# Opening of a hybrid mixer layer on one core: own slots for the rows of x, split loads, and one conditioning chunk multiplied on TensorE

## The reference

```
mod = c @ w_ada + b_ada                       # 6 x 1024: sh1, sc1, gt1, sh2, sc2, gt2
h   = rms_norm(x, g_mix) * (1 + sc1) + sh1
a, conv, linear, stick, gate_logits = split(h @ w_in)
merged = sum of sigmoid(gate_i) * branch_i     # window attention, convolution, GLA, stick-breaking
x = x + gt1 * (merged @ w_out)
h = rms_norm(x, g_mlp) * (1 + sc2) + sh2
x = x + gt2 * (relu(h @ w_up)**2 @ w_down)
```

## Time and profile before

| | |
|---|---|
| median of three runs | 1986.41 us (1985.16 to 1990.21) |
| the profiled execution | 1990.35 us, its span 1988.6 us |
| TensorE busy | 1927.7 us, 97% of the span |
| VectorE, ScalarE, GpSimd busy | 1191.7, 831.3, 227.2 us |
| bytes moved by DMA | 266.24 MB, mean 134 GB/s |
| mean granted TensorE clock | 0.992 |

### The profile page before, as it was taken

The page is one execution under the profiler, slowest core; times in us unless marked ns, Lnnn a source line. Parts: engine busy times, 40 slices in busy tenths (PEclk is TensorE's granted clock), DMA queues, the critical chain, the costliest instruction groups (busy, mean ns, idle before and its releaser), DMA issues. The chain is left out here.

```text
span 1988.6 us, 24178 instructions
## 1 busy us (share of the span) xinstructions
PE 1927.7 (97%) x9224; PEld 1551.3 (78%) x9224; DVE 1191.7 (60%) x1555; ACT 831.3 (42%) x1314; POOL 227.2 (11%) x136
## 2 busy tenths in 40 slices
PE   5999999999999999998999999999999999999999
PEld 4787888878766667876788788788788887888887
DVE  6545757101256666727657478667766765678855
ACT  5411111223466633164656255333455445444443
POOL 0121121211121225212101000000000000000000
PEclk9999999999999999999999999999999999999999
DMA  8345554323311242244122576501353546963343
GB/s 268 109 142 152 154 164 133 100 86 111 129 56 48 64 166 67 94 175 161 51 87 71 167 259 221 190 11 39 110 164 128 170 149 217 318 201 108 98 118 101
DMA packets 229004, 266.24 MB, mean 134 GB/s; under 512 B 12010, under 2 KB 157546, under 8 KB 228890
## 3 DMA queue, kind: packets, MB, share of 16 engines
q1 hardware_dynamic: 228720, 264.63, 42.0%
q10 hardware_dynamic: 170, 0.07, 0.0%
HBM read 187.46 MB, written 77.20 MB: 133 GB/s over the span
## 5 line engine op out<-in xcount | busy, mean ns | idle before, releaser
L663 PE MATMUL dn_ps<-h_hi,dn_hi 128*128 128x512 f32 (+1 forms) x1120 | 453.5, 405 | 16.0 <-ACT dn_out L156 5.1
L665 PE MATMUL dn_ps<-h_hi,dn_lo 128*128 128x512 f32 (+1 forms) x1120 | 440.2, 393 | 0.0
L664 PE MATMUL dn_ps<-h_lo,dn_hi 128*128 128x512 f32 (+1 forms) x1120 | 439.9, 393 | 0.0
L663 PEld LDWEIGHTS dn_ps<-h_hi,dn_hi 128*128 128x128 f32 (+1 forms) x1120 | 210.9, 188 | 84.2 <-issue 33.7
L156 ACT ACTIVATE dn_out<-dn_ps 128x512 f32<-128x512 f32 (+1 forms) x138 | 81.7, 592 | 424.1 <-PE dn_ps L665 402.8
L139 POOL TENSOR_TENSOR dn_lo<-dn_raw,dn_hi 128x1024 fp32r<-128x1024 f32 (+1 forms) x69 | 172.3, 2498 | 663.8 <-ACT dn_hi L135 663.8
L665 PEld LDWEIGHTS dn_ps<-h_hi,dn_lo 128*128 128x128 f32 (+1 forms) x1120 | 210.5, 188 | 47.9
L664 PEld LDWEIGHTS dn_ps<-h_lo,dn_hi 128*128 128x128 f32 (+1 forms) x1120 | 210.9, 188 | 43.1 <-issue 1.2
L1227 ACT ACTIVATE tl_ring_hi<-tl_cell 128x512 fp32r<-128x512 f32 x112 | 70.6, 630 | 140.7 <-PE mg_ps_y L665 126.5
L664 PE MATMUL mg_ps_y<-tl_ring_lo,tl_ring_hi 128*128 128x512 f32 x320 | 124.6, 389 | 0.0
L663 PE MATMUL mg_ps_y<-tl_ring_hi,tl_ring_hi 128*128 128x512 f32 x320 | 124.6, 389 | 0.0
(11 more groups left out here) (420 smaller groups left out, 3719.1 us busy)
## 6 DMA issues: line engine op xcount, KB each, us to landing
dn_raw<-w_in_dram SPq DMA_DIRECT2D x70, 512.0 KB, 4.3
tl_raw_hidden<-hidden SPq DMA_DIRECT2D x112, 256.0 KB, 2.7
ada<-w_ada_dram SPq DMA_DIRECT2D x24, 1024.0 KB, 8.0
proj<-dn_out SPq DMA_DIRECT2D x72, 256.0 KB, 2.3
logits<-dn_out SPq DMA_DIRECT2D x64, 256.0 KB, 2.3
tl_unit<-w_up_dram SPq DMA_DIRECT2D x64, 256.0 KB, 3.2
hidden<-tl_hidden_sum SPq DMA_DIRECT2D x16, 1024.0 KB, 4.9
tl_cell<-w_down_dram SPq DMA_DIRECT2D x64, 256.0 KB, 5.1
```

The costliest lines, as they stand in the source:

```text
L663: nc.tensor.matmul(out, w_hi[:, t, :], x_hi[:, t, :], start=begin, stop=False, skip_group_check=reopened)
L664: nc.tensor.matmul(out, w_hi[:, t, :], x_lo[:, t, :], start=False, stop=False, skip_group_check=reopened)
L665: mm = nc.tensor.matmul(out, w_lo[:, t, :], x_hi[:, t, :], start=False, stop=end, skip_group_check=reopened)
```

## The change

- Each row tile of x has a slot of its own: four in the old place, four in the space that the low part of h takes later (`x_lent`). No load of x waits.
- ScalarE's queue issues c and six of the vectors before `root(0)`; the other seven loads are issued by SP between x's fifth tile and the first chunk.
- A chunk is loaded in two halves of four pieces each, with a semaphore each.
- GpSimd scales rows 1 to 5 (`x_pooled`), VectorE rows 0, 6 and 7.
- Chunk 1 is not chained on VectorE: TensorE multiplies its 32 blocks of 128x128 by the columns of c and accumulates them in PSUM (`direct`), 16 blocks ahead of `opening(0)` and 16 behind it, where `sum_chunk(1)` stood. Chunks 0, 2 and 3 are chained as before.
- On ScalarE the splits of the first weight tiles move behind the roots, the third into the loop over f. On VectorE chunk 0's chain, the vectors' copies, `modulation(0)` and `scale_columns(0)` move ahead of the last takes, and the low parts of the first weight tiles behind them.

```
-X_RING = 4
+X_OWN = 4
+X_ON_POOL = 5
...
+    PART = KT // 2
+    DIRECT = ((1, 0), (1, 1))
...
+        x_lent = nc.alloc_sbuf_tensor_at("x_lent", [P, S // P - X_OWN, D], F32, offset=k.h_base + 3 * KT * S * 2)
...
+            def load_chunk(n, part):
+                slot, rows = n % ADA_RING, slice(part * PART, (part + 1) * PART)
+                if n >= ADA_RING and part == 0:
+                    sp.wait_ge(ada_direct, direct_until(n - ADA_RING))
+                    if chained(n - ADA_RING):
+                        sp.wait_ge(ada_step, steps_until(n - ADA_RING))
...
+            for tt in range(1, X_ON_POOL + 1):
+                pool.wait_ge(x_rooted, tt + 1)
+                nc.gpsimd.tensor_scalar(x_rows(tt), x_rows(tt), rinv_x[:, tt:tt + 1], None, ALU.mult).then_inc(x_pooled, 1)
...
+            root(0)
+            root(1)
+            root(2)
+            take(0)
+            root(3)
+            take(1)
...
+            root(7)
+            take(5)
+            dense.split(act, 0)
+            take(6)
+            dense.split(act, 1)
+            take(7)
             for f in range(KT):
...
+                if f == 0:
+                    act.wait_ge(turned, 2 * TT)
                 nc.scalar.activation(k.h_hi[:, f, :], xn[:, f, :], ACT.Identity, **affine).then_inc(h_hi_ready, 1)
...
+                if f == 0:
+                    dense.split(act, 2)
...
+            def direct(n, part):
+
+                pe.wait_ge(ada_in[2 * (n % ADA_RING) + part], 32 * (n // ADA_RING + 1))
+                if n >= 1:
+                    pe.wait_ge(mod_ready, n)
+                closes = not chained(n)
+                for i, first in enumerate(CHUNKS[n]):
+                    for m in range(ADA_COLS):
+                        for kt in range(part * PART, (part + 1) * PART):
+                            opens = part == 0 and i == 0 and m == 0 and kt == 0
+                            last = nc.tensor.matmul(ps_m[:, first + m:first + m + 1], ada[:, n % ADA_RING, kt, i, m * P:(m + 1) * P],
+                                                    k.cols[:, V_C + kt:V_C + kt + 1], start=opens, stop=(closes and kt == KT - 1 and m == ADA_COLS - 1 and i == len(CHUNKS[n]) - 1))
+                last.then_inc(ada_direct, 1)
...
+            turn(5)
+            if chained(0):
+                sum_chunk(0)
+            turn(6)
+            turn(7)
+            if (1, 0) in DIRECT:
+                direct(1, 0)
             for f in range(KT):
                 opening(f)
-                if f % 2 == 0 and f // 2 + 1 < OPEN_CHUNKS:
+                if f == 0 and (1, 1) in DIRECT:
+                    direct(1, 1)
+                elif f % 2 == 0 and f // 2 + 1 < OPEN_CHUNKS:
                     sum_chunk(f // 2 + 1)
```

More of the change, by code:

```diff
@@ L235, in sum_after, with direct_until, chained, steps_until @@
         return load_step(i) + 2
+    def direct_until(n):
+        return sum(1 for chunk, part in DIRECT if chunk <= n)
+    def chained(n):
+        return [kt for kt in range(KT) if (n, kt // PART) not in DIRECT]
+    def steps_until(n):
+        return sum(len(chained(i)) for i in range(n + 1))
+    def sums_until(n):
+        return sum(1 for i in range(n + 1) if chained(i))
     with ExitStack() as ctx:
@@ L473, in sum_chunk @@
                         at = (i * ADA_COLS + m) * P
-                        last = nc.tensor.matmul(ps_m[:, first + m:first + m + 1], ada_sum[:, at:at + P], k.ones[:, 0:1], start=True, stop=True)
+                        last = nc.tensor.matmul(ps_m[:, first + m:first + m + 1], ada_sum[:, at:at + P], k.ones[:, 0:1], start=alone, stop=(alone or at == (len(CHUNKS[n]) * ADA_COLS - 1) * P))
                 last.then_inc(ada_done, 1)
+            def direct(n, part):
[10 more added lines that the diff above has]
+                last.then_inc(ada_direct, 1)
             def opening(f):
@@ L495, in _ @@
             pe.wait_ge(const_ready, 2)
-            for tt in range(TT):
-                turn(tt)
-                if tt == 1:
-                    pe.wait_ge(c_in, 16)
-                    nc.tensor.transpose(ps_v[:, 0:KT], c_rows[:, :], k.ident[0:KT, 0:KT]).then_inc(c_turned, 1)
+            turn(0)
+            pe.wait_ge(c_in, 16)
+            nc.tensor.transpose(ps_v[:, 0:KT], c_rows[:, :], k.ident[0:KT, 0:KT]).then_inc(c_turned, 1)
+            turn(1)
+            turn(2)
+            turn(3)
+            pe.wait_ge(c_taken, 1)
+            if (0, 0) in DIRECT:
+                direct(0, 0)
+            turn(4)
             pe.wait_ge(vec_in, 16 * n_vec)
-            pe.wait_ge(vec_taken, 1)
             nc.tensor.transpose(ps_v[:, 0:P], vec_rows[:, :], k.ident[:, :])
@@ L529, in scale_rows @@
                 dve.wait_ge(x_rooted, tt + 1)
-                nc.vector.tensor_scalar(x_rows[:, tt % X_RING], x_rows[:, tt % X_RING], rinv_x[:, tt:tt + 1], None, ALU.mult).then_inc(x_scaled, 1)
+                nc.vector.tensor_scalar(x_rows(tt), x_rows(tt), rinv_x[:, tt:tt + 1], None, ALU.mult).then_inc(x_scaled, 1)
             def take(tt):
@@ L539, in chain @@
                 late = n - OPEN_CHUNKS
-                if first == 0:
-                    if late >= 0:
-                        dve.wait_ge(late_in[late % LATE_RING], 16 * (late // LATE_RING + 1))
-                    else:
-                        dve.wait_ge(ada_in[n % ADA_RING], 32 * (n // ADA_RING + 1))
-                    if n >= 1:
-                        dve.wait_ge(ada_done, n)
-                for kt in range(first, last):
+                own = chained(n)
+                for at, kt in enumerate(own):
+                    if not first <= kt < last:
+                        continue
+                    if kt == own[0] and late >= 0:
+                        dve.wait_ge(late_in[late % LATE_RING], 16 * (late // LATE_RING + 1))
+                    if late < 0 and (kt == own[0] or kt == PART):
+                        dve.wait_ge(ada_in[2 * (n % ADA_RING) + kt // PART], 32 * (n // ADA_RING + 1))
+                    if kt == own[0] and sums_until(n) > 1:
+                        dve.wait_ge(ada_done, sums_until(n) - 1)
                     ck = k.cols[:, V_C + kt:V_C + kt + 1]
@@ L594, in _ @@
                     nc.vector.memset(k.headsum[64 * a:64 * a + 64, 64 * b:64 * b + 64], 1.0 if a == b else 0.0)
[L595 to L611 removed]
+            scale_rows(0)
+            dve.wait_ge(c_turned, 1)
+            nc.vector.tensor_copy(k.cols[:, V_C:V_C + KT], ps_v[:, 0:KT]).then_inc(c_taken, 1)
+            dve.wait_ge(c_taken, 1)
+            take(0)
+            take(1)
+            chain(0, 0, 1)
+            take(2)
+            chain(0, 1, 3)
+            take(3)
+            chain(0, 3, KT)
+            take(4)
+            scale_rows(6)
             dve.wait_ge(vec_turned, 1)
```

147 lines of the change are left out of this document (76 added, 71 removed).

## The result

Over 22 runs of each, the kernel after took 1991.21 us in the median (1986.05 to 1994.5) and the one before 1987.23 (1981.73 to 1991.66). The ratio is 1.0017, with a 95% interval of 1.0009 to 1.0025: the change makes this kernel slower by 0.17%, some 3.4 us (the medians lie 4.0 apart). Forecast were 1984.7 us, 1.7 less than before, in a range of 1980.3 to 1989.5. The profiled execution took 1994.22 us, its span 1992.4.

The account below looks back on a forecast made before the run. It took the opening's end to set the total: blocks from 27.9, plus 7.1, 6.4 and 4.4 us, put chunk 1's modulation at 45.8, a gain of 1.7. From the median 1986.41 that gave 1984.7 us, range 1980.3 to 1989.5.

Parts of the forecast that it names:

- What bounds the kernel: Whole kernel: TensorE is busy 494.75 of 500 us behind the opening, so only when the opening ends counts.
- A microsecond out of the opening is one out of the total: Behind the opening: the rest runs as long as before, so time saved in the opening shortens the total equally.
- h nine microseconds earlier: Ahead of the first product: h_hi at about 27.5 instead of 36.51, its low part at 31.2 instead of 40.20.
- Where the blocks start: TensorE's first blocks of chunk 1: start at 27.9 us, when the first half of chunk 1 has landed.
- the term of GpSimd's rows: Five row scalings in the opening: taken as 1.3 us each, hidden up to about 2.1, so zero in the sum.
- The rival with the other sign: GpSimd's five rows slow: blocks start at 15.9 + 5p, late from p = 2.4; at most 10.3 us slower; chance 0.06.
- Hidden, as forecast: VectorE in the opening: GpSimd's scalings may hold it 1.3 us each, covered by chunk 0's wait for its load.
- The level of the first sixteen blocks: Blocks ahead of opening(0): run at the low clock, 7.1 us, ending at 35.0.
- The second sixteen blocks: Blocks behind opening(0): run at the high clock, 4.4 us, ending at 45.8.
- its first rival: The clock falls in the second sixteen blocks: gain 1.7 becomes 0.4 or a loss up to 1.7; chance 0.32.
- the forecast's opening: Opening as a whole: chunk 1's modulation at 45.8 instead of 47.58, later periods unchanged, a gain of 1.7 us.

Follow-up runs that it names:

- rows_on_vector: Kernel after, with VectorE scaling all eight rows of x and GpSimd none; ratio to the kernel before 0.9998.
- second_chained: Kernel after, with the second half of chunk 1 chained on VectorE again instead of the second sixteen blocks; ratio to the kernel before 0.9987.
- fillers: Kernel after, with an unused product of 512 columns behind each of the second sixteen blocks; ratio to the kernel before 1.0026.
- eight_blocks: Kernel after, with VectorE scaling all rows, eight blocks of chunk 1 on TensorE and its other six pieces chained; ratio to the kernel before 0.9964.
- own_slots: Kernel before, with only eight own slots for the rows of x; ratio to the kernel before 1.0001.
- before_again: Kernel before, unchanged, timed and profiled once more; ratio to the kernel before 0.9994.
- all_chained: Kernel after, with chunk 1 chained entirely on VectorE and no blocks; ratio to the kernel before 0.9989.
- rows_vector_second_chained: Kernel after, with VectorE scaling all rows and chaining chunk 1's second half, first sixteen blocks kept; ratio to the kernel before 0.9985.

## Why the prediction was wrong

**What bounds the kernel**: held in direction. Behind the opening the rates are the same, and the kernels with an opening 4 to 9 us shorter are the faster ones. "A microsecond out of the opening is one out of the total" held among the changed kernels to within 2.6 us, and not against the kernel before, as told under what stays open.

**h nine microseconds earlier**: nearly. `h_hi` came 6.9 us earlier, at 29.65, and its low part was ready at 33.66; the forecast had 27.5 and 31.2. The 2.1 us are those of GpSimd's rows: without them `h_hi` came at 27.54, in `rows_on_vector`. Nothing waited for h in the kernel after.

**Where the blocks start**: 27.9 was forecast, and measured were 27.98 without GpSimd and 29.32 with it. The step that failed is the term of GpSimd's rows, which I had left out of the sum as hidden, at 1.3 us a row. A row took 2.83 to 3.08 us. The rival with the other sign had the mechanism, `turn(5)` behind five rows that stand in a line, and put the point at which it shows at 2.4 us a row; I gave it 0.06. With the measured rows, 14.6 us for the five, its formula gives 30.5 for the blocks; they came at 29.32, since a turn or a sum took 1.6 to 1.8 us in the row and not 1.9 to 2.0. I had leaned on the memset's 1811 ns for 2048 columns, a thing that reads nothing, when the nearest rows that read a tile were 2528 ns for 1024 columns and 1192 ns for 256. The Trainium skill, GPSIMD Engine Reference (Engine selection), says that one-input work there is roughly at line rate; here it was 2.83 us against VectorE's 0.75 for the same tile, nearly four times as long, and the measurement decides.

Row work beside it costs VectorE something too. The chain's steps with GpSimd's rows beside them, then those of chunks 2 and 3 without (count, busy us, mean ns of one):

```profile
L636 DVE SCALAR_TENSOR_TENSOR ada_sum<-ada,cols,ada_sum 128x512 f32<-128x512 f32 x7 | 6.6, 950 | 0.2
```
```profile
L636 DVE SCALAR_TENSOR_TENSOR ada_sum<-ada,cols,ada_sum 128x512 f32<-128x512 f32 x14 | 10.5, 750 | 0.5
```

A step took 950 ns instead of 750. Hidden, as forecast: the chain had been done before the last takes.

**The level of the first sixteen blocks**: right, 6.69 us where 7.1 was forecast (0.41 less). In two other profiles with the same instructions ahead of them (`second_chained` and `fillers`) they ran at the high level, at 0.12 us a record, and ended 3 us sooner; so that the level was as forecast in both profiles of the kernel after is in part luck.

**The second sixteen blocks**: here the prediction failed a second time, by what it named as its first rival (0.32). They were priced at 4.4 at the high level with nothing behind them; they took 4.72, and the clock fell within them. The period behind them then took 11.19 us instead of 10.06, VectorE's slack of 0.4 gone. Against the forecast that is 0.32 and 1.13 us. The fall cost more, 2.30 us by `rows_on_vector`, and the rival had 1.3 to 1.5 for one behind the blocks, up to twice that for one that starts in them. The difference is a wrong price: at the high level the sixteen took 3.49 us and not 4.4. The earlier trace rows had that, too: the product behind the sum of 46.59 starts at 47.40, 0.10 us a record, where I had divided the time until VectorE's next step.

**The sum of it**: from the forecast's opening, 1.7 us shorter, to the measured one, 1.28 longer, are 2.98 us. Blocks late +1.42, first sixteen -0.41, `opening(0)` +0.39 (6.79 instead of 6.4, the clock rose 5.26 us behind its start, not 4.99), second sixteen +0.32, modulation +0.18, the period behind +1.13: 3.03.

**What stays open.** The two profile pairs show 1.3 and 1.5 us of longer opening, the ratio some 3.4 (1.8 to 5.0). Behind the opening low stretches of 3.4 to 13.7 us come at much the same places in nearly all profiles (in that of before at 713.6, 932, 973, 1086 and 1417 us and at the end); their lengths differ, and some profiles have one or two more: 34.35 us of low level in all in the profile of before and 25.10 in its repetition, 38.11 and 34.15 in those of after, 17.67 in `rows_on_vector`. About half of that is lost time, and it moves the total by several microseconds either way: without the opening the thirteen spans lie between 1902.6 and 1910.9 us, and with half of the low time taken off as well between 1890.6 and 1894.0. Before is at 1891.2 and 1894.0 there, after at 1891.8 and 1893.5, so I find no other loss behind the opening in the profiles.

The times say a little more. Taken against the kernel after, the ratios follow the openings within 2.6 us. Taken against the kernel before, all ten profiles of changed kernels, `eight_blocks` too, come with a time 0.9 to 4.7 us above what the opening says (2.1 for the kernel after), while `own_slots` and `before_again` come at 0.0 and -1.0. The interval of each is about 2 us to either side, but the sign is the same ten times. So something that all changed kernels share, such as the new order of loads, may cost about 2 us that the profiled executions don't show, or their clock falls more often in the executions that were not profiled. One profile is a thin base for that: those of before and after lie 3 us above their medians, those of `second_chained` and `rows_on_vector` 4.5 us below. No run here settles it.

## What to carry to other kernels

Work given to an idle engine is only free up to the length of its idle time: with the rows on VectorE the opening ended at 74.67 us with no blocks, 71.70 with eight, 73.75 with sixteen and 77.91 with thirty-two, and the gap that they were to fill was 4.2 us. Price an operation on another engine by the nearest rows that read and write the same kind of tile there, and if the break point lies between two candidate rows, treat it as undecided. The clock can fall in a stretch of one-column matmuls, and most of the bill may come in the work behind them, so look at the spacing of the products behind the edit, not at the edit alone. Take more than one profile before a fall is put down to an edit: here the same blocks kept the clock in one kernel and lost it in another.

## What the runs showed of the hardware

- **Transposes can raise the clock.** In `second_chained` the eight transposes at 27.68 took 1.91 us and the blocks at 29.38 ran at 0.12 us a record, 1.00 from 29.50 on: the clock rose behind transposes and a sum. In `rows_on_vector` eight transposes took 1.09 us at 18.57, behind twenty-four without a gap from 10.29 on, and 1.97 where the level is low. I had read from the earlier trace rows that they don't raise it, and the Trainium skill, TensorE: Matmul & The Clock Gate (PE-mode transpose), says the same; these two profiles speak against both. In the kernel after the same transposes stood without a gap too, and the clock rose only at 41.27, so the runs don't tell when they do.
- **One-column matmuls have two prices.** A record took 0.21 to 0.22 us at 1.2 GHz (6.83 us for 32, 13.65 for 64) and 0.11 to 0.12 at 2.4 GHz (3.63 and 3.76 for 32).
- **The clock fell in stretches of them, while TensorE was busy throughout**: at 44.7 us in the kernel after and near 44.8 in its repetition, at 32.8 in `second_chained` and 32.9 in `fillers`. It did not in `rows_on_vector` (3.63 us of them) and not with products between them. These times the low level lasted 6.8 us.
- **It fell without blocks, too**: behind a wait of 2.39 us and a sum of 1.05 in `all_chained`, and behind a wait of 0.89 and a sum in `rows_vector_second_chained`, for 3.4 us each. Waits of 0.4 us ahead of such a sum did no harm in either profile of before.
- **GpSimd's scaling of 128x1024 by a column took 2.83 to 3.08 us**, and slowed VectorE's steps of two tile operands from 750 to 950 ns, without stopping them; beside a subtraction of GpSimd's a VectorE step had been held for the whole 2.43 us.
